# Six matmul steps of the last gate tile issued inside the first sample's latent attention, and that sample's key transposes issued two prompt steps earlier

## Chip, cores and metric

One core of a Trainium2 chip runs the whole kernel. The time is what the device needs for one execution, in microseconds (us). Each core has five engines with their own instruction streams: TensorE (PE, matmuls, with PEld its weight loads), VectorE (DVE), ScalarE (ACT), GpSimd (POOL) and SyncE (SP). They wait for one another on semaphores, and an instruction that waits holds up all that stands behind it on its engine.

## What is computed

One inference step of a decoder of two layers, for a prompt of 256 tokens and for 8 samples of 8 new tokens each, all in float32. A layer is a gated FFN, a mixing part, and a second gated FFN, with norms around each. The mixing part has three branches (a delta-rule recurrence A, a dilated window attention B, a latent attention C), and

```
gates = sigmoid(h @ w_in[gate columns] + b_gate)     # 3 x 1024 channels
m = gates[0] * (ya @ w_a) + gates[1] * (yb @ w_b) + gates[2] * (yc @ w_c)
x += post_mix(m @ w_out)
```

Branch C for a sample attends over 2048 past latent rows, which lie in pages that are gathered through a table, and over its own 8 tokens:

```
s = q_lat . ckv_all + q_rope . krope_all ;  p = softmax(s * scale) ;  o_lat = p @ ckv_all
```

## The kernel before, in words

The work of a layer is in one hand-written order on each engine: `ffn("f1")`, `a_proj`, `rwkv`, `bc_proj`, `sw_prompt`, `sw_sample`, `latent_prep`, `ml_prompt`, `ml_sample`, `mix`, `ffn("f2")`. The change touches the last part of `ml_prompt` (latent attention of the prompt) and the first of `ml_sample` (latent attention of the 8 samples).

**Dealt steps.** The gate and branch products are filler for PE. They are 40 tiles of 128 channels by 320 tokens: tiles 0 to 7 gate, 8 to 15 branch A, then 8 gate, 8 branch B, 8 gate. A gate tile is 8 steps (one matmul of 128x320 each over the 8 slices of the model width; a step shows as two MATMUL instructions in the trace), a branch tile 4, 256 steps in all (`N_DEAL`). `deal(count, cap)` issues the next `count` steps and stops at `cap`. Tile i accumulates in PSUM bank 6 + i % 2. The last step of a gate tile raises the semaphore `pgm`; ACT then takes the tanh of the tile (`gates_out`, L1660) and raises `gate`. So the 24th gate tile is done with `pgm` 24 and read out with `gate` 24. It lies in bank 7.

**ml_prompt.** `prompt(...)` runs 17 iterations n = 0 to 16 on PE: scores of unit n + 2, half of the dealt steps (3 of 6), values of unit n - 1, two transposes of unit n (L711), the other 3 steps. Before `ml_prompt` 154 steps have been dealt; the 17 times 6 here end at 256. In the last two iterations no scores are left. DVE (`prompt_attention`) runs i = 0 to 18: it masks and takes the maximum of unit i (L2256), divides unit i - 1 (L2289), copies the transposed shares of unit i - 2 (L2300), copies the output of unit i - 3 (L2271, `finish`, which raises `prompt_y`). At i = 17 and 18 it also calls `keys(0, 0)` and `keys(0, 1)`.

**keys(b, high)** (L2418) transposes the gathered pages of sample b in 32x32 blocks: two transposes of 128x1024 for the lower half of the latent channels, and two of 128x1024 and one of 128x512 for the upper half and the rotary keys. The lower half first waits for the three gathers of sample b (`s_kr`).

**ml_sample.** PE first waits for `prompt_y` 32, `ml_prep`, `gate` 24, `br_ev` and `s_ql`, then issues `own_tokens(0)` and for each sample b: `scores(b)`, `by_channel(b-2)`, `own_tokens(b+1)`, `values(b-1)`, `shares(b, 0)`, `shares(b, 1)`. `shares` transposes the exponentials (8 transposes, L711, and one small one, of the own tokens' shares, into bank 7 columns 448 to 511) and waits for `ml_exp` b + 1. The order on DVE is

```
own_scores(0)
for b in range(NB):
    if b:
        keys(b + 1, 0)
        divisor(b - 1)
    maximum(b)
    own_scores(b + 1)
    if b == 0:
        keys(1, 0)
    ...
    keys(b + 1, 1)
```

with `maximum` L2471 to L2477, `own_scores` L2466, `own_share` L2485 (after the keys; it raises `ml_p`, for which the small transpose waits), `divisor` L2490 to L2494. ACT takes the exponentials (L1736 and L1738), copies the outputs (L1744) and the transposed shares (L1749, L1750).

**Page gathers on POOL** (L690 the rotary keys, L693 two of latent rows; 3 per sample). There are four buffers; those of samples 2 and 3 lie in `ring` and `h`, and the first 4096 columns of `ring` hold the weights of the gate tiles 20 to 23 until `pgm` 24. POOL goes in this order, and the change leaves it as it is:

```
elif b == 1:
    pool.wait_ge(S["prompt_mm"], 2 * H + 16)
elif b in (2, 3):
    pool.wait_ge(S["prompt_y"], 2 * H + 16)
    pool.wait_ge(S["pgm"], 24)
else:
    pool.wait_ge(S["ml_pv"], b - 3)
```

(each of the first two with a wait for `ml_prep` too).

Of the kernel before, what the change touches and what calls it, by code (L numbers as in the profile page):

```python
# [189 lines left out]
N_DEAL = 2 * (64 + 32) + 64  # L190
# [78 lines left out]
def build(nc, io):  # L269
    SCB, SCC = DH ** -0.5, (DNOPE + DROPE) ** -0.5  # L270
    with ExitStack() as ctx:
# [150 lines left out]
        S = {n: sem(n) for n in STEPS}  # L422
# [275 lines left out]
        def _(pe):  # L698
# [396 lines left out]
            def prompt(base, scores, rows, count, cap):  # L1095

                def values(n):
                    hd, r0 = n % H, 64 * (n % 2)
                    pe.wait_ge(S["prompt_pt"], base + n + 1)
                    if n >= 2:  # L1100

                        pe.wait_ge(S["prompt_y"], base + n - 1)
                    for i in range(n // H + 1):
                        q = mm(ps[r0:r0 + 64, 5, P * (n % 2):P * (n % 2) + P], rows[:, i, hd * 64:hd * 64 + 64], PTp[n % 2][:, i, :], i == 0, i == n // H)
                    q.then_inc(S["prompt_o"], 1)

                scores(0)
                scores(1)
                for n in range(17):
                    if n + 2 < 16:  # L1110
                        scores(n + 2)
                    deal(count // 2, cap)
                    if n:
                        values(n - 1)
                    if n < 16:
                        pe.wait_ge(S["prompt_p"], base + n + 1)
                        for i in range(n // H + 1):
                            q = tr(ps[:, 4, i * P:i * P + P], Pc[n % 2][:, i * P:i * P + P])
                        q.then_inc(S["prompt_T"], 1)
                    deal(count - count // 2, cap)  # L1120

            def sw_prompt():
                pe.wait_ge(S["qk_ev"], 16)
# [204 lines left out]
            def ml_sample():  # L1328
                pe.wait_ge(S["prompt_y"], 2 * H + 16)
                pe.wait_ge(S["ml_prep"], 1)  # L1330
                pe.wait_ge(S["gate"], 24)
                pe.wait_ge(S["br_ev"], 2 * KD)

                pe.wait_ge(s_ql, 16 * 12)
# [17 lines left out]
                def own_tokens(b):  # L1352

                    if b >= NB:
                        return
                    if b:
                        pe.wait_ge(S["ml_own"], b)
                    if b >= 4:
                        pe.wait_ge(S["ml_olT"], b - 3)
                    o = ps[0:NS, 6, 0:TS]  # L1360
                    tk = slice(SEQ + TS * b, SEQ + TS * b + TS)
                    for c in range(2):
                        mm(o, QL[:, c, NS * b:NS * b + NS], ckvT[:, c, tk], c == 0, False)
                    mm(o, QR[64:96, b, :], ckvT[64:96, 2, tk], False, True).then_inc(S["ml_s"], 1)

                def shares(b, r):

                    if r == 0:
                        pe.wait_ge(S["ml_exp"], b + 1)
                    if b:  # L1370
                        pe.wait_ge(S["ml_pt"], 2 * b - 1 + r)
                    for u in range(4):
                        q = tr(ps[:, 4 + r, u * P:u * P + P], Pl[:, (4 * r + u) * P:(4 * r + u) * P + P])
                    if r:
                        pe.wait_ge(S["ml_p"], b + 1)
                        if b:
                            pe.wait_ge(S["ml_osb"], b)
                        q = tr(ps[0:NS, 7, 448:512], PnL, NS)
                    q.then_inc(S["ml_PT"], 1)
# [26 lines left out]
                for b in range(NB):  # L1406
                    scores(b)
                    by_channel(b - 2)
                    own_tokens(b + 1)
                    values(b - 1)  # L1410
                    for r in range(2):
                        shares(b, r)
# [60 lines left out]
        def _(act):  # L1473
# [179 lines left out]
            def gates_out(upto):  # L1653

                for n in range(gates_done[0], upto):
                    gates_done[0] = n + 1
                    bank = 6 + (n % 8 + 16 * (n // 8)) % 2
                    dst = (mt, gb, gc)[n // 8][:, n % 8, :]
                    act.wait_ge(S["pgm"], n + 1)
                    act.activation(dst, ps[:, bank, 0:T], ACT.Tanh, scale=0.5, bias=pp("b_gate", n)).then_inc(S["gate"], 1)  # L1660
# [60 lines left out]
            def ml_prompt():  # L1721
                for n in range(16):
                    act.wait_ge(S["prompt_nm"], 2 * H + n + 1)
                    scores = Sp[n % 2][:, 0, 0:(n // H + 1) * P]
                    act.activation(scores, scores, ACT.Exp, scale=SCC, bias=sml[:, 2 + n % 2:3 + n % 2], accum_out=sml[:, 4 + n % 2:5 + n % 2]).then_inc(S["prompt_e"], 1)
                    gates_out(complete(DEAL_AT["ml"] + DEAL_ML * n, "gate"))
                gates_out(24)

            def ml_sample():

                def exponentials(b):
                    act.wait_ge(S["ml_nm"], b + 1)
                    if b:

                        act.wait_ge(S["ml_PT"], 2 * b)
                    act.activation(Pl.rearrange("p (u i k) -> p i u k", u=8, i=4), ps[:, 0:4, 0:256].rearrange("p i (u k) -> p i u k", u=8),  # L1736
                                   ACT.Exp, scale=SCC, bias=sml[:, 4:5], accum_out=sml[:, 8:9])
                    act.activation(Pown[b % 2], Pown[b % 2], ACT.Exp, scale=SCC, bias=sml[0:NS, 4:5], accum_out=sml[0:NS, 10:11]).then_inc(S["ml_exp"], 1)  # L1738

                def output(b):  # L1740
                    if b < 0:
                        return
                    act.wait_ge(S["ml_pv"], b + 1)
                    act.activation(Osb, ps[:, 7, 0:KV_LORA], ACT.Copy).then_inc(S["ml_osb"], 1)  # L1744

                def shares_out(b, r):
                    act.wait_ge(S["ml_PT"], 2 * b + r + 1)
                    if r:
                        act.activation(PTl, ps[0:NS, 7, 448:512], ACT.Copy)  # L1749
                    act.activation(PTL[:, 4 * r:4 * r + 4, :], ps[:, 4 + r, :].rearrange("p (t n) -> p t n", t=4), ACT.Copy).then_inc(S["ml_pt"], 1)  # L1750

                for b in range(NB):
                    exponentials(b)
                    output(b - 1)
                    for r in range(2):
                        shares_out(b, r)
                output(NB - 1)
# [22 lines left out]
        def _(dve):  # L1780
# [480 lines left out]
            def prompt_attention(tag, y, one_group):  # L2261
# [13 lines left out]
                for i in range(19):  # L2275
# [25 lines left out]
                        dve.wait_ge(S["prompt_pt"], base + n + 1)  # L2301
                    if 3 <= i < 19:
                        finish(i - 3)
                    if one_group and i in (17, 18):
                        dve.wait_ge(S["pgm"], 20)
                        keys(0, i - 17)
                    branches_out(complete(DEAL_AT["ml"] + DEAL_ML * (i - 1), "branch") if one_group else min(KD, complete(DEAL_AT["sw"] + DEAL_SW * (i - 1), "branch")))

            branches_done = [0]
# [296 lines left out]
```

## Time and profile before

| | us |
|---|---|
| median of 3 runs | 2690.97 (2684.81 to 2694.35) |
| the profiled execution | 2691.49 |
| its span in the trace | 2689.6 |
| PE busy | 2589.1 (96%) |
| DVE busy | 1358.1 (50%) |
| ACT busy | 522.0 (19%) |
| POOL busy | 67.2 (2%) |

The span runs from the first to the last instruction that the profile records; the device time of the same execution is 1.9 us more. Busy time is an average over stages with different limits. The chain that ended last is followed back from the last instruction to what released each one; the timeline gives each engine's instructions in order of time, with the idle time before a group and what ended it in square brackets; times count from the start of the span. Layer 0's `ml_sample` begins near 936 us, layer 1's near 2269 us. PEclk in the table of windows is the granted clock of TensorE, 1.00 for 2.4 GHz and 0.50 for 1.2 GHz.

### The profile page before, as it was taken

The page shows a single profiled execution, that of the slowest core. Times are in us where ns is not written, and L with a number is a line of the kernel's source. Part 1 is how long each engine was busy: PE and PEld are TensorE (multiplying, and loading weights), DVE is VectorE, ACT ScalarE, POOL GpSimd, SP SyncE. Part 2 cuts the span into 40 slices and gives each one's busy share as a digit, 9 for nine tenths or more (in the row PEclk, how much of TensorE's full clock was granted, in tenths as well). Part 3 has the DMA queues.
Part 4 walks back from the last instruction along what each step waited for, and adds up shares of the span by engine and source line. Part 5 has one row for each costly group of instructions (what it writes and reads, how often), then busy time and mean ns, then how long its engine had stood idle before and what let it go on. Part 6 is the DMA issues. An engine that isn't in the chain of part 4 may idle for free.

```text
span 2689.6 us, 52084 instructions
## 1 busy us (share of the span) xinstructions
PE 2589.1 (96%) x22652; PEld 2042.4 (76%) x22652; DVE 1358.1 (50%) x2927; ACT 522.0 (19%) x1109; POOL 67.2 (2%) x92
## 2 busy tenths in 40 slices
PE   7999999999989999999999999999999899999998
PEld 6999656656656667899989996566566666779998
DVE  5663553436542482665376534533455435717653
ACT  2110131121432121211021111211224211312110
POOL 0000000000000110000000000000000001100000
PEclk9999999989999999999999999999999999999999
DMA  6435578631981379544534456684329614794442
GB/s 224 155 103 166 187 244 323 224 114 56 383 313 63 105 262 366 161 128 118 161 120 141 122 163 222 245 317 160 128 102 380 255 63 161 264 350 137 142 108 85
DMA packets 258754, 505.61 MB, mean 188 GB/s; under 512 B 9760, under 2 KB 196512, under 8 KB 243424
## 3 DMA queue, kind: packets, MB, share of 16 engines
q1 hardware_dynamic: 249824, 330.83, 37.4%
q0 software_dynamic: 8704, 171.45, 17.3%
q8 instruction: 180, 2.95, 0.4%
q14 instruction: 46, 0.38, 0.0%
HBM read 491.95 MB, written 140.85 MB: 235 GB/s over the span
## 4 chain that ended last, share of the span: by engine, by line
PE 90%; DVE 4%; ACT 2%; DMA 2%; issue 1%; SPq 0%; DVEq 0%; ACTq 0%
PE ps L708 84%; PE ps L711 6%; DMA ring<-in_w_in_dram 1%; DMA ring<-in_f_wu_dram 1%; ACT big L1680 1%; ACT reg L1680 0%; DMA big<-in_cache_swa_k_dram 0%; DVE reg L1843 0%; DVE reg L2053 0%; DVE x L1854 0%; SPq L572 0%; DVE ring L2380 0%; DVE big L2187 0%; DVE reg L2352 0%; ACT reg L1572 0%
## 5 line engine op out<-in xcount | busy, mean ns | idle before, releaser
L708 PE MATMUL ps<-reg 128*128 128x160 f32 (+12 forms) x4584 | 534.8, 292 | 3.1 <-issue 1.6
L708 PEld LDWEIGHTS ps<-reg 128*128 128x128 f32 (+5 forms) x4584 | 470.0, 163 | 50.5 <-issue 34.2
L708 PE MATMUL ps<-h,ring 128*128 128x320 f32 (+3 forms) x1792 | 464.7, 408 | 29.9 <-DMA ring<-in_f_wu_dram 13.8
L708 PE MATMUL ps<-reg,ring 128*128 128x160 f32 (+2 forms) x2912 | 458.2, 312 | 0.0
L708 PEld LDWEIGHTS ps<-reg,ring 128*128 128x128 f32 (+1 forms) x2912 | 415.5, 189 | 26.7 <-issue 6.2
L708 PEld LDWEIGHTS ps<-h,ring 128*128 128x128 f32 (+2 forms) x1792 | 311.6, 194 | 134.4 <-issue 45.5
L708 PE MATMUL ps<-ring,h 128*128 128x512 f32 (+3 forms) x896 | 249.9, 474 | 2.7 <-DMA ring<-in_w_in_dram 2.7
L708 PE MATMUL ps<-big,ring 64*64 64x64 f32 (+3 forms) x1920 | 231.7, 292 | 12.3 <-ACT big L1502 6.7
L708 PEld LDWEIGHTS ps<-big,ring 128*128 128x128 f32 (+1 forms) x1920 | 189.2, 165 | 63.3 <-issue 39.9
L708 PEld LDWEIGHTS ps<-ring,h 128*128 128x128 f32 (+1 forms) x896 | 104.0, 165 | 83.6 <-issue 64.6
L708 PE MATMUL ps<-big,reg 32*64 32x256 f32 (+8 forms) x2144 | 132.1, 346 | 0.0
L708 PEld LDWEIGHTS ps<-big,reg 32*64 32x64 f32 (+4 forms) x2144 | 101.7, 134 | 23.8 <-issue 14.8
L711 PE MATMUL ps<-cst,big 128*128 128x128 f32 (+1 forms) x672 | 98.8, 284 | 17.6 <-ACT big L1680 7.3
L708 PE MATMUL ps<-ring 128*16 128x128 f32 (+3 forms) x1888 | 98.7, 272 | 3.2 <-DVE ring L2380 3.2
L711 PEld LDWEIGHTS ps<-cst,big 128*128 128x128 f32 (+1 forms) x672 | 72.3, 140 | 38.4 <-ACT big L1680 12.4
L708 PEld LDWEIGHTS ps<-ring 128*16 128x16 f32 (+3 forms) x1888 | 76.9, 116 | 25.0 <-issue 18.6
L711 PE MATMUL ps<-cst,reg 128*128 128x128 f32 (+3 forms) x436 | 73.7, 289 | 12.7 <-ACT ring L1738 6.1
L708 PE MATMUL ps<-ring,reg 32*64 32x256 f32 (+2 forms) x1312 | 81.8, 398 | 0.0
L1547 ACT ACTIVATE reg<-ps 128x320 f32<-128x320 f32 x40 | 17.5, 437 | 323.1 <-PE ps L708 323.1
L708 PE MATMUL ps<-ys,ring 128*128 128x320 f32 x256 | 77.4, 437 | 0.0
L711 PEld LDWEIGHTS ps<-cst,reg 128*128 128x128 f32 (+3 forms) x436 | 50.5, 143 | 34.3 <-issue 12.9
L1982 DVE TENSOR_TENSOR ys<-ys,ps 128x320 f32<-128x320 f32 x40 | 19.5, 488 | 109.7 <-PE ps L708 109.6
(311 smaller groups left out, 2673.1 us busy)
## 6 DMA issues: line engine op xcount, KB each, us to landing
out_o_swa_k_s_dram<-in_cache_swa_k_dram POOLq DMA_DIRECT2D x16, 4080.0 KB, 15.6
out_o_swa_v_s_dram<-in_cache_swa_v_dram POOLq DMA_DIRECT2D x16, 4080.0 KB, 16.6
ring<-in_w_in_dram SPq DMA_DIRECT2D x30, 2048.0 KB, 8.7
ring<-in_f_wd_dram SPq DMA_DIRECT2D x32, 1408.0 KB, 7.2
ring<-in_f_wg_dram SPq DMA_DIRECT2D x42, 1024.0 KB, 5.4
ring<-in_f_wu_dram SPq DMA_DIRECT2D x42, 1024.0 KB, 8.1
big<-in_cache_swa_k_dram SPq DMA_DIRECT2D x32, 1024.0 KB, 8.4
ring<-in_cache_swa_v_dram SPq DMA_DIRECT2D x32, 1024.0 KB, 6.9
```

The costliest lines, as they stand in the source:

```text
L708: return pe.matmul(out, lhsT, rhs, start=first, stop=last, skip_group_check=True)
L711: return pe.transpose(out, in_, ident[0:rows, 0:rows])
L1547: act.activation(GU[u % 2][:, :, 0, 0:HT], summed(X), ACT.Copy).then_inc(S["gu_act"], 1)
L1680: act.activation(KTw[n % 2][:, c, 0:w], ps[:, 4 + c % 2, 0:w], ACT.Copy).then_inc(S["kt_act"], 1)
L1982: dve.tensor_tensor(Vs, Xc, Y, ALU.add).then_inc(S["gu_sum"], 1)
```

## The change

Both calls of `deal` in `prompt` stop six steps earlier when they serve `ml_prompt`. The six steps (2 to 7 of the last gate tile) are issued in `ml_sample`, after `scores(0)` and `own_tokens(1)` and ahead of `shares(0, 0)`. The wait for `gate` 24 ahead of `ml_sample` becomes one for 23, and a wait for 24 stands ahead of the small transpose of sample 0, which writes the same bank. ACT reads the tile out after sample 0's exponentials. DVE issues `keys(0, 0)` and `keys(0, 1)` at i = 15 and 16.

```diff
@@ prompt, PE
-                    deal(count // 2, cap)
+                    deal(count // 2, cap - (6 if cap == N_DEAL else 0))
...
-                    deal(count - count // 2, cap)
+                    deal(count - count // 2, cap - (6 if cap == N_DEAL else 0))
@@ ml_sample, PE
-                pe.wait_ge(S["gate"], 24)
+                pe.wait_ge(S["gate"], 23)
...
                     if r:
                         pe.wait_ge(S["ml_p"], b + 1)
+                        if b == 0:
+                            pe.wait_ge(S["gate"], 24)
...
                     own_tokens(b + 1)
+                    if b == 0:
+                        deal(N_DEAL)
                     values(b - 1)
@@ ml_prompt, ACT
-                gates_out(24)
+                gates_out(23)
@@ ml_sample, ACT
                     exponentials(b)
+                    if b == 0:
+                        gates_out(24)
                     output(b - 1)
@@ prompt_attention, DVE
-                    if one_group and i in (17, 18):
+                    if one_group and i in (15, 16):
                         dve.wait_ge(S["pgm"], 20)
-                        keys(0, i - 17)
+                        keys(0, i - 15)
```

## Rows read from the trace of the kernel before

**Rows 1.** The page's first part, the whole span: busy time, share, instructions.
```profile
PE 2589.1 (96%) x22652; PEld 2042.4 (76%) x22652; DVE 1358.1 (50%) x2927; ACT 522.0 (19%) x1109; POOL 67.2 (2%) x92
```

**Rows 2.** The chain that ended last, both layers: start us, us, what.
```profile
935.09 0.78 issue
...
956.92 9.37 PE ps L708 x188
...
2267.79 0.78 issue
...
2291.10 9.16 PE ps L708 x187
```

**Rows 3.** Timeline, layer 0, end of ml_prompt and first sample: start us, us, what.
```profile
921.66 0.28 DVE L2271 COPY ys<-ps 64x128 f32<-64x128 f32 x1
...
925.85 0.29 DVE L2271 COPY ys<-ps 64x128 f32<-64x128 f32 x1
...
929.30 3.40 PE L708 MATMUL ps<-h,ring 128*128 128x320 f32 x12
929.57 0.42 DVE L2300 COPY ring<-ps 128x256 f32<-128x256 f32 x1 [3.43 <-PE ps L711]
...
930.35 2.37 DVE L2418 STREAM_TRANSPOSE ring<-big 128x1024 f32<-128x1024 f32 x2
...
932.63 0.65 PE L708 MATMUL ps<-ring 128*64 128x128 f32 x4
...
933.21 1.88 PE L708 MATMUL ps<-h,ring 128*128 128x320 f32 x6
933.32 0.29 DVE L2271 COPY ys<-ps 64x128 f32<-64x128 f32 x1 [0.60 <-PE ps L708]
933.65 2.97 DVE L2418 STREAM_TRANSPOSE big<-big 128x1024 f32<-128x1024 f32 x3
935.13 0.53 ACT L1660 ACTIVATE ys<-ps,par 128x320 f32<-128x320 f32 x1 [4.56 <-PE ps L708]
```

**Rows 4.** Timeline, PE's hole in the first sample of layers 0 and 1.
```profile
943.97 1.09 PE L711 MATMUL ps<-cst,reg 128*128 128x128 f32 x8 [3.06 <-ACT ring L1738]
...
2276.94 1.97 PE L711 MATMUL ps<-cst,reg 128*128 128x128 f32 x8 [3.02 <-ACT ring L1738]
```

**Rows 5.** Timeline of POOL: gathers of sample 2, layer 0 (first, third), layer 1 (first).
```profile
935.89 0.95 POOL L690 DMA_INDIRECT ring<-in_cache_mla_krope_dram,pidx  x1 [13.66 <-PE ps L708]
...
938.39 0.94 POOL L693 DMA_INDIRECT ring<-in_cache_mla_ckv_dram,pidx  x1 [0.30 <-issue]
...
2268.59 0.95 POOL L690 DMA_INDIRECT ring<-in_cache_mla_krope_dram,pidx  x1 [13.65 <-PE ps L708]
```

**Rows 6.** DMA queues: sample 1's bytes; its third gather, us to landing; all of layer 0.
```profile
q0 software_dynamic: 368, 2.36, 56.6%
...
reg<-in_cache_mla_ckv_dram,pidx POOLq DMA_INDIRECT x1, 7.8
...
DMA to landing us min/median/max: 6.4/7.2/8.2
```

**Rows 7.** Timeline, second sample: DVE's keys of sample 2, the maximum, what follows.
```profile
947.96 2.33 DVE L2418 STREAM_TRANSPOSE ring<-ring 128x1024 f32<-128x1024 f32 x2
...
951.43 1.20 DVE L2473 TENSOR_REDUCE sml<-ps 128x1 f32<-128x1024 f32 x1
951.48 3.67 PE L708 MATMUL ps<-big,reg 128*64 128x256 f32 x32
...
956.68 0.10 PEld L711 LDWEIGHTS ps<-cst,ring 64*64 64x64 f32 x1 [0.17 <-DVE ring L2485]
...
2285.32 1.23 DVE L2473 TENSOR_REDUCE sml<-ps 128x1 f32<-128x1024 f32 x1 [0.85 <-PE ps L708]
```

**Rows 8.** Windows: us, PE, PEld, DVE, ACT, POOL busy, PEclk, DMA share, GB/s.
```profile
944.00:949.00 5.00, 4.97 (x89) 3.40 (x97) 4.96 (x6) 1.30 (x3) 0.00 (x0) 0.66 1.02 428
2276.00:2284.00 8.00, 7.06 (x121) 5.02 (x129) 7.82 (x12) 2.18 (x7) 0.00 (x0) 0.57 0.94 371
1087.00:1092.00 5.00, 4.53 (x11) 2.98 (x12) 4.95 (x13) 5.00 (x13) 0.00 (x0) 0.66 0.93 298
...
2421.00:2427.00 6.00, 5.49 (x21) 3.93 (x22) 5.00 (x13) 6.00 (x16) 0.00 (x0) 1.00 0.87 285
```

## The prediction, made before the changed kernel was run

> **What bounds the kernel now.** The page's first part comes first: PE is busy in 96% of the span [rows 1], so time is saved where PE stands idle or runs at the lower clock, and lost where it gets a new wait. The chain that ended last shows the two places at the seam of `ml_prompt` and `ml_sample` (layer 0; layer 1 repeats it). PE waits 0.78 us at 935.09 [rows 2], for the tanh of gate tile 23 at 935.13 [rows 3]. Then, after scores(0) and own_tokens(1), it is idle 3.06 us up to 943.97 until ACT's exponentials are there; layer 1 has 3.02 us [rows 4]. The change aims at both: six steps are to leave the first place and fill the second. The windows show what else the hole costs: in the stretches behind it the granted clock is 0.66 over 5 us and 0.57 over 8 us [rows 8], that is partly the 1.2 GHz level. Last the timeline of POOL and DVE, for all that waits for the steps that move: POOL issues sample 2's gathers at 935.89, 0.80 us after the dealt steps' end at 935.09 [rows 2, 5]. It cannot go before `pgm` 24.
>
> **Removed from the prompt's end.** The group of 12 matmuls at 929.30 is six steps, two instructions a step; three of them stay, three go. values(15) followed it at 932.63 [rows 3], so twelve take 3.33 us and values(15) moves 1.66 us forward, to 930.97. The 6 matmuls of 933.21 (1.88 us) go too. What then releases `ml_sample` is DVE's copy of values(15), at 933.32 for 0.29 us [rows 3]: now done at 931.95. I add 0.25 us for the wait's release and the satisfied waits behind it (after the tanh's end at 935.66, PE needed 0.21 to 935.87 [rows 2, 3]). PE starts `ml_sample` at 932.20 instead of 935.87: **3.67 us earlier**. The wait for `gate` 23 costs nothing; that tile is finished before the moved tile's first step.
>
> **Keys at i = 15 and 16.** 2.37 and 2.97 us of DVE [rows 3] stand now behind the output copies that end at 921.94 and 926.14. The first lasts to 924.31, the division of unit 15 moves behind it, and PE asks for that only at its transposes near 929. The second ends at 929.11, and DVE's next copy starts at 929.57 [rows 3]. Cost: nothing, hidden by DVE's idle 3.43 us; with that cover gone it would be at most these 5.3 us. They also no longer hold up anything at the end; the page wait of sample 0 and `pgm` 20 are long met.
>
> **Added in the first sample.** own_tokens(1) ended at 943.97 - 3.06 = 940.91, now at 937.24. Six steps take 1.88 + 1.66 = 3.54 us, to 940.78. The exponentials are there at 943.97 - 3.67 = 940.30, so the first shares come 0.5 us later than they could. ACT's tanh (0.53 us) fits behind the exponentials, before the first copy of shares. If nothing else happened, sample 1 would begin some 3.2 us earlier and at full clock.
>
> **What is late next: the pages of sample 2.** `pgm` 24 now comes at 940.78 where it came at 935.09. With the same 0.80 us lag POOL's first gather starts at 941.58, 5.7 us later than in the old kernel, while all else is 3.7 us earlier. The third gather starts 938.39 - 935.89 = 2.50 us behind the first [rows 5]. It has no landing time in the trace, so I take its nearest neighbour, the third gather of sample 1, of equal shape: 7.8 us [rows 6]. Together 10.3 us after the first issue: 951.88. The ends are 9.7 (median 7.2) and 10.7 (maximum 8.2) [rows 6]. The check on it: in the old kernel this gives 946.2, and DVE did take up these pages at 947.96 with no idle time [rows 7].
>
> DVE meets keys(2, 0) in sample 1's turn **ahead of** divisor(0) and maximum(1). Queued behind that wait are the maximum, so ACT's exponentials, so PE's shares(1), own_share(1) and with it scores(2). From the start of keys(2, 0) to the maximum is 951.43 - 947.96 = 3.47 us [rows 7]: now at 951.88 + 3.47 = 955.35, **3.92 us later than in the old kernel**. The small transpose ahead of scores(2) was waiting for DVE [rows 7], so scores(2), at 956.92 [rows 2], follows the maximum by 5.49 us: 960.84, +3.92.
>
> Layer 1: the hole ended 2276.94 - 3.02 = 2273.92, so the pieces there are 0.3 us longer. First gather at 2268.59 + 5.69 + 0.31 = 2274.59 [rows 5], pages at 2284.89, maximum at 2288.36 where it was 2285.32 [rows 7], scores(2) at 2293.85 where it was 2291.10 [rows 2]: +2.75. It is less because the old maximum waited 0.85 us for a slow-clocked PE.
>
> **The clock.** PE has finished values(0) near 950.4 (scores(1) starts near 942 and takes some 4.1 us at full clock, own tokens 0.5, values 3.67 [rows 7]) and stands idle until the exponentials at about 958.8: 8 us instead of 3. After the 3 us holes the clock rows lost (1 - 0.66) x 5 = 1.7, (1 - 0.57) x 8 = 3.4 with 0.9 of idle in it, and 1.7 us [rows 8]; a fourth stretch, 2421 to 2427, behind a like pause, shows 1.00 and lost nothing. The old holes' loss is already in the old times above, since the new wait swallows whatever is gained before it. The new hole's loss comes on top, less what passes while DVE is still at work on sample 2's keys, some 2 us of clock time. Bounds 0 and 2.4 us a layer; I take 1.3, between, since a longer pause is nearer to the stretches that lost.
>
> **Sum.** +3.92 + 2.75 + 2 x 1.3 = +9.3 us on the profiled execution's 2691.49, that is 2700.8; the median stands 0.5 lower, so **2700.3**. From there on each sample is PE's own pace (9.37 us of matmuls without a break in the chain [rows 2]), so nothing is caught up. Ends: stalls of 3.3 + 2.1 with landing at 9.7, less 0.5 each if POOL's lag is nearer to 0.3, and no clock loss: +4.4. Stalls of 4.3 + 3.2 and 2.4 twice: +12.3.
>
> **Rivals.** (B) The hole is filled and the pages don't matter. Then DVE reaches maximum(1) 3.67 us earlier in layer 0 and, free of the slow PE, 4.6 in layer 1, and scores(2) follows: -3.7 and -4.9, together -8.6 us, 2682.4. It decides at the start of keys(2, 0): the pages would have to be there at 947.96 - 3.67 = 944.29, 2.7 us after the first issue. Break-even is 947.96. For it: the hole and the low clock are real [rows 4, 8]. Against it: 2.36 MB [rows 6] at 428 GB/s [rows 8] alone take 5.5 us. Only if I misread which gather is held by `pgm` 24 does it stand. Chance 0.10.
> (C) The gathers land much sooner than sample 1's, because they overlap. If all three are there 7.2 us after the first issue, the median of a single one [rows 6], the pages come at 948.78 and 2281.79, the maximum at 952.25 (+0.8) and 2285.26 (-0.1); with 2.6 of clock that is +3.3, 2694.3 for the median. At the bound of 5.5 us the maximum is 0.9 and 1.8 us earlier than in the old kernel, and with 0 to 2.6 us of clock the time is 2688 to 2691. For it: the lag of the first bytes may hide behind the other gathers. Against it: sample 1's own three landings. Chance 0.10, all within 0.3%.
> The Trainium skill (DMA: Bandwidth & Descriptors, Anatomy of one DMA) has a transfer issued by GpSimd take 2.0 us plus its bytes at 436 GB/s. For 2.36 MB that is an estimate of 7.4 us in place of 10.3, and 2694.7 in place of 2700.3. The trace disagrees with it for sample 1's gathers: three issues 1.25 us apart put the last landing at 10.3.
> (A) is my forecast, the chain as worked out: chance 0.80.
>
> **From cases to numbers.** About 0.3%, 8.1 us, is what a measurement of this kernel can tell from no change: the lines are 2682.9 and 2699.0. (A) runs from 2695.4 to 2703.3; two thirds of it lies over 2699.0 (clock loss of over some 1.4 us in all, at the middle stalls): slower 0.52, same 0.28. (C) adds 0.10 to same. (B) lies on the lower line: 0.07 faster, 0.03 same. The range takes in (A), (C)'s upper half and about a microsecond of scatter: 2691 to 2705.
>
> **What would show it.** Right, if in the new trace POOL's first gather of sample 2 starts near 941.6 and 2274.6; DVE waits for DMA for some 7 us before keys(2, 0) in both layers; maximum(1) starts near 955.4; PE is idle about 8 us ahead of shares(1) with a lower clock behind it; and `ml_sample` begins near 932.2. The key transposes at i = 15 and 16 should move no PE row. Wrong, if DVE goes into keys(2, 0) without idle time, if the hole at 943.97 stays, if ml_sample starts no earlier, or if later samples run faster than before and win the stall back.

## The result, and the profile after

The changed kernel is slower: 2703.61 us, the median of 20 executions, beside 2695.11 for 20 of the old kernel on the same chip. The ratio on record is 1.0048 [1.0032, 1.0064], that is +13 us, from +9 to +17. It is not the quotient of the two medians, which is 1.0032 (+8.5 us); in the runs below the two also differ, by up to 0.2%. Every ratio here is the one on record, with its interval. The profiled execution took 2702.42 us, 10.9 more than the one of before. The forecast was +9.3 us on that execution; its time, 2700.3, is 3.3 us under the median measured now. It was built on a median of 3 executions, 2690.97, which stands 4.1 us under that of 20.

The page's first part, of the changed kernel (beside [rows 1]):

```profile
PE 2587.9 (96%) x22652; PEld 2042.3 (76%) x22652; DVE 1357.3 (50%) x2927; ACT 521.2 (19%) x1109; POOL 67.3 (2%) x92
```

No engine has more or less to do. What was added is waiting, and the timeline of layer 0 has it. (Line numbers in the kernel after are 4 higher in ACT's part and 6 higher in DVE's.)

```profile
923.93 0.42 DVE L2306 COPY ring<-ps 128x256 f32<-128x256 f32 x1 [0.37 <-PE ps L711]
...
926.55 0.40 PE L708 MATMUL ps<-reg 128*64 128x8 f32 x4 [0.46 <-DVE ys L2277]
...
931.55 3.50 PE L708 MATMUL ps<-h,ring 128*128 128x320 f32 x12
...
934.89 1.04 PE L711 MATMUL ps<-cst,reg 128*128 128x128 f32 x8
935.09 0.53 ACT L1664 ACTIVATE ys<-ps,par 128x320 f32<-128x320 f32 x1 [0.46 <-PE ps L708]
...
935.85 0.95 POOL L690 DMA_INDIRECT ring<-in_cache_mla_krope_dram,pidx  x1 [19.19 <-PE ps L708]
936.03 1.98 PE L708 MATMUL ps<-ring,reg 32*64 32x256 f32 x64
...
938.35 0.94 POOL L693 DMA_INDIRECT ring<-in_cache_mla_ckv_dram,pidx  x1 [0.30 <-issue]
...
946.73 2.37 DVE L2424 STREAM_TRANSPOSE ring<-ring 128x1024 f32<-128x1024 f32 x2 [7.98 <-DMA ring<-in_cache_mla_ckv_dram,pidx]
...
950.23 1.21 DVE L2479 TENSOR_REDUCE sml<-ps 128x1 f32<-128x1024 f32 x1
...
953.72 1.97 PE L711 MATMUL ps<-cst,reg 128*128 128x128 f32 x8 [8.38 <-ACT ring L1742]
...
955.86 3.71 PE L708 MATMUL ps<-ring,reg 32*64 32x256 f32 x64
```

Read from above: `ml_sample` starts (926.55) as soon as DVE has copied values(15); the twelve matmuls of the moved steps stand where the hole of [rows 4] was, and the shares follow them without idle time (934.89). POOL's first gather of sample 2 comes 0.8 us behind the steps. DVE then stands 7.98 us before it may transpose sample 2's first keys, maximum(1) queues behind that, and PE is idle 8.38 us. The 64 matmuls that take 1.98 us at 936.03 take 3.71 at 955.86. The chain that ended last has the gathers in it, which that of before has not:

```profile
935.85 0.79 POOL ring L690
936.64 0.47 issue
937.11 0.94 POOL ring L693
938.05 0.30 issue
938.35 8.35 DMA ring<-in_cache_mla_ckv_dram,pidx
```

Layer 1 repeats it (timeline; beside the last lines of [rows 5, 4, 7]):

```profile
2270.80 0.95 POOL L690 DMA_INDIRECT ring<-in_cache_mla_krope_dram,pidx  x1 [19.18 <-PE ps L708]
...
2284.90 1.21 DVE L2479 TENSOR_REDUCE sml<-ps 128x1 f32<-128x1024 f32 x1
...
2288.39 1.97 PE L711 MATMUL ps<-cst,reg 128*128 128x128 f32 x8 [8.10 <-ACT ring L1742]
```

The windows behind the new holes (columns as in [rows 8]). While PE takes up work again, at 953.72, the granted clock is 0.50, the 1.2 GHz level. In the next 5 us it is 0.60, and 0.54 in layer 1: still the lower level for most of the time. The 5 us after these are at full clock in both layers.

```profile
951.00:956.00 5.00, 2.28 (x17) 1.83 (x25) 4.78 (x12) 2.38 (x7) 0.00 (x0) 0.50 1.02 424
956.00:961.00 5.00, 5.00 (x120) 3.38 (x128) 2.84 (x8) 0.67 (x2) 0.00 (x0) 0.60 0.05 20
2290.00:2295.00 5.00, 5.00 (x99) 3.08 (x103) 3.47 (x11) 0.84 (x3) 0.00 (x0) 0.54 0.20 82
```

**A ruler for the seam.** Two executions drift apart by some microseconds before the seam is reached, with the same code (its first mark below stands at 929.57 in the old trace and at 923.93 in the new). So all that follows counts from DVE's copy of unit 15's transposed shares, the first line of the timeline above. Each column is the start of one line of the timeline, less that mark, layer 0 / layer 1; max(b) is DVE's maximum of sample b, "wait" DVE's idle time for sample 2's pages. "Gather 2" is POOL's first gather of sample 2, and SP's first transfer in the two plain kernels. The number behind a name is the chip's.

| kernel, chip | ml_sample | gather 2 | max(0) | max(1) | max(2) | wait |
|---|---|---|---|---|---|---|
| before, first pair | 6.3 / 6.3 | 6.3 / 6.3 | 10.9 / 11.2 | 21.9 / 23.1 | 31.5 / 33.0 | 0 |
| after, first pair | 2.6 / 2.6 | 11.9 / 11.9 | 7.2 / 7.2 | 26.3 / 26.0 | 38.2 / 37.9 | 8.0 / 7.7 |
| again2 (= after), 7 | 2.6 | 11.9 | 7.3 / 7.3 | 26.2 / 26.2 | 38.2 / 38.1 | 7.9 / 7.9 |
| thin_base, 7 | 6.3 | 6.3 | 10.9 / 10.9 | 22.7 / 21.9 | 32.7 / 31.7 | 0 |
| thin_after, 7 | 2.6 | 11.9 | 7.3 / 7.2 | 22.2 / 22.2 | 33.5 / 32.7 | 3.9 / 3.9 |
| late_order, 7 | 5.5 | 10.9 | 10.2 / 10.1 | 20.9 / 20.9 | 33.3 / 33.3 | 0 |
| plain_base, 8 | 6.3 | 5.6 | 10.9 / 13.1 | 22.7 / 24.0 | 32.7 / 33.7 | 0 |
| plain_after, 8 | 2.6 | 11.2 | 7.2 / 7.2 | 24.0 / 24.1 | 35.3 / 35.3 | 5.5 / 5.8 |
| base (= before), 11 | 6.3 | 6.3 | 19.1 / 19.3 | 30.8 / 31.2 | 42.9 / 43.3 | 0 |
| keys_only, 1 | 6.4 | 6.4 | 19.1 / 19.2 | 31.0 / 31.1 | 43.0 / 43.1 | 0 |
| again (= after), 1 | 2.6 | 11.9 | 7.3 / 7.3 | 26.0 / 24.9 | 39.0 / 36.8 | 7.7 / 6.5 |
| late_gather, 1 | 6.3 | 11.7 | 10.9 / 10.9 | 25.0 / 25.2 | 35.7 / 35.0 | 3.0 / 3.3 |
| free_pages, 1 | 2.6 | 2.8 | 15.2 / 15.6 | 26.2 / 26.6 | 36.8 / 37.2 | 0 |

### The profile page after: what moved, and what is told of

Read it like the earlier page. It is cut to its first block, busy times and chain, and to the rows that moved or that the text cites. A ratio compares the mean times of both kernels' runs of the same rounds, so it can differ in the third digit from the quotient of the medians.

```text
span 2700.5 us, 52086 instructions
## 1 busy us (share of the span) xinstructions
PE 2587.9 (96%) x22652; PEld 2042.3 (76%) x22652; DVE 1357.3 (50%) x2927; ACT 521.2 (19%) x1109; POOL 67.3 (2%) x92
## 3 DMA queue, kind: packets, MB, share of 16 engines
q1 hardware_dynamic: 249824, 330.83, 37.2%
## 4 chain that ended last, share of the span: by engine, by line
PE 90%; DVE 4%; ACT 2%; DMA 1%; issue 1%; SPq 0%; POOL 0%; DVEq 0%; POOLq 0%; ACTq 0%
PE ps L708 85%; PE ps L711 6%; DMA ring<-in_f_wu_dram 1%; DMA ring<-in_cache_mla_ckv_dram,pidx 1%; ACT big L1684 1%; ACT reg L1684 0%; DVE ring L2386 0%; DVE reg L1849 0%; DVE reg L2059 0%; DVE x L1860 0%; DVE big L2193 0%; DVE ring L2424 0%; SPq L572 0%; DVE reg L2358 0%; ACT reg L1576 0%
## 5 line engine op out<-in xcount | busy, mean ns | idle before, releaser
L711 PE MATMUL ps<-cst,reg 128*128 128x128 f32 (+3 forms) x436 | 73.6, 288 | 23.3 <-ACT ring L1742 16.5
```

The costliest lines, as they stand in the source:

```text
L711: return pe.transpose(out, in_, ident[0:rows, 0:rows])
```

## Experiments

Theory P, the forecast's: the pages of sample 2 come late, and that is the loss. Its rival R (S in the expectations): the moved steps, or the keys in their new place, cost in themselves. Where an expectation names a time without a chip, it goes by the first pair.

### First group: the pages, the keys, and the kernel itself

**again** is the changed kernel, unchanged, for a common footing.

> The changed kernel once more. Theory P (late pages): DVE waits for sample 2's pages for about 8 us in both layers, and the maximum of sample 2 starts 38.4 us after the last full group of dealt steps where it was 31.8 in the old kernel (33.3 in layer 1); 9 to 14 us slower than the old kernel. What the changed kernel's layer 1 lost beyond that (PE's issue gaps of 2.58 and 0.6 us in samples 6 and 7) is there again if it belongs to the change, and absent or elsewhere if it is scatter of one execution.

Measured: 2723.98 beside 2730.09 for the old kernel, ratio 0.9976 [0.9958, 0.9994]. The sign is turned, and both kernels are 20 to 35 us slower than in the first pair.

**keys_only**: the old kernel with `i in (15, 16)` and `keys(0, i - 15)`.

> The old kernel with DVE's key transposes of sample 0 at i = 15 and 16 and nothing else. Both theories: the start of ml_sample hangs on the tanh of the last gate tile, so nothing moves on PE: within 1 us of the old kernel. If the earlier transposes did hold PE up in the prompt's last units, it would show here as 1 us or more.

Measured: 2735.06, 0.9999 [0.998, 1.0018]. The seam stands where it stands in base, to 0.2 us, so no cost of the keys' new place shows; the interval of the time is some 5 us to either side.

**late_gather**: the old kernel, with POOL's gathers of sample 2 held back as the change does, and no step moved:

```diff
                         pool.wait_ge(S["pgm"], 24)
+                        pool.wait_ge(S["ml_mm"], 1)
```

> The old kernel, no step moved; POOL's gathers of samples 2 and 3 also wait for the end of sample 0's scores, some 4.7 us later than before. Theory P: pages near 951.2 in the old kernel's clock instead of 946.2, maximum of sample 1 some 3.3 us later than in the old kernel, a second hole of PE of 3 to 5 us ahead of its shares and low clock behind it: 5 to 11 us slower in all, though nothing but the gathers is late. Rival S (the moved steps themselves, or the cover they gave, cost the time): no change within 1 us.

Measured: 2722.18, 0.9968 [0.9949, 0.9988]. The wait for the pages is there (3.04 us), and yet it is faster, where 5 to 11 us of loss were expected.

**free_pages**: the changed kernel, where the last six steps no longer read the slot that sample 2's pages are to fill, so that POOL may go at once:

```diff
-                        pool.wait_ge(S["pgm"], 24)
+                        pool.wait_ge(S["pgm"], 23)
...
+                        if n >= N_DEAL - 6:
+                            q = mm(out, kvup[1][:, 0:P], x[:, k, :], ...)
```

> The changed kernel, but the six moved steps multiply other data that lie in SBUF anyway (lora's first 128 columns and x), and POOL's gathers of samples 2 and 3 wait for pgm 23; the last gate tile's values are other ones. Same matmuls in the same places, pages free of them. Theory P: no wait for pages before keys(2, 0), no hole of 3 us in sample 0 and no low clock behind it: 7 to 11 us faster than the old kernel, so some 20 faster than the changed one. Rival S: as slow as the changed kernel.

Measured: 2721.02, 0.9959 [0.9941, 0.9977], and no page wait; but max(0) comes at 15.2 instead of 7.3.

What follows: on this chip, gathers issued early cost time in the first sample, gathers issued late cost a wait in the second. In the old kernel max(0) is at 19.1 here and 10.9 in the first pair, with the same code. That cost wasn't in either theory. So this group does not tell P from R for the loss of the first pair.

### Second group: a second chip of this kind, and the order of DVE

**base** is the old kernel, with a profile.

> The old kernel, for its trace beside the others of this group. After the first group there are two theories. P (late pages): the wait of DVE for sample 2's pages is what the change costs. F (starved PE): PE's own instructions come slowly while page gathers run, which shows as idle time ended by issue between small groups of weight loads; in the kernel with only the keys moved this held the scores of sample 0 up by 8 us, in the changed kernel the gathers start after these scores. F expects on a chip that behaves as that one: the first maximum 19 us after the copy of unit 15, later samples 12.7 us apart. On one that behaves as in the first two traces: 10.9 us, and 10.6 us apart.

Measured: 2732.82, 0.9993 [0.9973, 1.0012]. Its timeline of POOL and of PE's weight loads shows the loss:

```profile
932.69 0.95 POOL L690 DMA_INDIRECT ring<-in_cache_mla_krope_dram,pidx  x1 [13.65 <-PE ps L708]
...
938.94 0.94 POOL L693 DMA_INDIRECT h<-in_cache_mla_ckv_dram,pidx  x1 [0.30 <-issue]
```

```profile
933.02 1.18 PEld L708 LDWEIGHTS ps<-ring,reg 32*64 32x64 f32 x38
934.74 0.22 PEld L708 LDWEIGHTS ps<-ring,reg 32*64 32x64 f32 x6 [0.54 <-issue]
935.50 0.23 PEld L708 LDWEIGHTS ps<-ring,reg 32*64 32x64 f32 x6 [0.54 <-issue]
936.97 0.20 PEld L708 LDWEIGHTS ps<-ring,reg 32*64 32x64 f32 x4 [1.25 <-issue]
...
940.62 0.17 PEld L708 LDWEIGHTS ps<-big,reg 32*64 32x64 f32 x1 [0.45 <-issue]
941.33 0.81 PEld L708 LDWEIGHTS ps<-big,reg 32*64 32x64 f32 x23 [0.53 <-issue]
```

From 1.5 us after POOL's first gather has started to 1.5 us after its last has ended, PE gets a handful of matmuls at a time, then 0.45 to 1.25 us nothing, and waits for no engine ("issue"). In the first pair the same scores run beside gathers with no such gap: 64 matmuls in 1.98 us at 936.03, in the first timeline.

**order**: the changed kernel, DVE's maximum(1) and own_share(1) put ahead of keys(2, 0):

```diff
-                        keys(b + 1, 0)
+                        if b != 1:
+                            keys(b + 1, 0)
...
-                    if b == 0:
-                        own_share(0)
+                    if b < 2:
+                        own_share(b)
+                    if b == 1:
+                        keys(2, 0)
```

> The changed kernel with one more edit on DVE: in sample 1's turn keys(2, 0) stands behind the maximum and own_share(1) instead of ahead of them. Theory P: DVE still waits for the pages, but the maximum of sample 1 comes some 6 to 8 us earlier, PE's hole ahead of shares(1) goes, and a shorter one of 2 to 4 us stands ahead of scores(2): 4 to 6 us per layer faster than the changed kernel, 8 to 12 in all. If the time is lost elsewhere: no change against the changed kernel.

Measured: 2725.71, 0.9964 [0.9945, 0.9982]. The page wait is gone, but max(1) comes at 24.7 and 25.1 where again, on chip 1, had 26.0 and 24.9. The expected 6 to 8 us are missed: it is 1.3 us sooner in layer 0 and no sooner in layer 1. DVE now waits for PE, whose scores(1) stand in the gathers' stretch:

```profile
949.44 1.23 DVE L2479 TENSOR_REDUCE sml<-ps 128x1 f32<-128x1024 f32 x1 [8.61 <-PE ps L708]
```

**steps_only**: the changed kernel with the keys back at i = 17 and 18.

> The changed kernel with the key transposes of sample 0 back at i = 17 and 18. They stand ahead of the copy of unit 15 that releases ml_sample and ahead of scores(0)'s upper half: ml_sample starts some 1 us later and scores(0) waits for keys: the first maximum 1 to 3 us later than in the changed kernel, and the gathers' start with it; 2 to 4 us slower than the changed kernel.

Measured: 2724.18, 0.997 [0.9954, 0.9986]. Here the keys do matter: `ml_sample` starts at 3.5 instead of 2.6 and max(0) comes at 8.5 instead of 7.3, but the page wait (7.0 us) swallows it. In their new place the keys hold nothing up: in the first timeline DVE even stands idle for 0.37 us behind them, ahead of the copy at 923.93. In the old place they would hold the earlier seam up by 1.2 us.

**tanh_wait**: the old kernel with the keys at 15 and 16 and the wait for tile 23 instead of 24 ahead of `ml_sample` (24 only ahead of the small transpose); no step moved.

> The old kernel with its keys at i = 15 and 16 and PE's wait for the last gate tile's tanh moved behind the shares of sample 0, all steps where they were. pgm 24 and the gathers come when they came, ml_sample starts 0.5 to 0.8 us earlier: 1 to 1.5 us faster than the old kernel in all, nothing else moves. It takes the part of the gain that does not delay the pages.

Measured: 2729.81, 0.9985 [0.9965, 1.0004]: not told apart from no change. In its trace `ml_sample` starts at 5.5 instead of 6.3, POOL's gather stays at 6.4. That is 0.8 us a layer, the issue row of [rows 2]; at max(0) 0.3 to 0.5 us of it are left (18.8 beside base's 19.1 and 19.3).

### Third group: a chip like the first pair's

**thin_base** and **thin_after**: the kernels before and after, the latent-row gathers of samples 2 and 3 replaced by as many gathers of 2 KB rows, so that a third of sample 2's bytes is left, with the same issues. What these two samples attend to is then wrong.

```diff
+                        if b in (2, 3):
+                            pool.indirect_dma_start(out=KRc[b % 4][half][:, 0:2, :]..., in_=krope, in_offset=rows_of(0))
+                            continue
```

> The old kernel, but the latent-row gathers of samples 2 and 3 fetch 2 KB a row from the rotary-key cache in place of 8 KB of latent rows (0.79 MB a sample, not 2.36); the rest of these two samples' pages is stale, so the two samples' attention is not computed from their keys. As many gathers, issued at the same times, with a third of the bytes. Theory F says that bytes in flight starve PE's instruction supply: on a chip like that of the groups before, the first maximum comes 11 to 14 us after the copy of unit 15 instead of 19.1, in both layers, and the kernel is 10 to 16 us faster than the old one. If the issue on POOL or the number of gathers did it: 19, and no faster.

Measured: 2692.78, 0.9995 [0.9967, 1.0023].

> The changed kernel with the same thin gathers for samples 2 and 3. The pages land some 6 us after the first issue instead of 10.7. Theory P: DVE's wait shrinks to about 2 to 3 us, the second maximum comes about 21 us after the copy of unit 15 instead of 24.9 to 26, and PE's issue gaps in sample 1's scores shrink too; 4 to 10 us faster per layer than the changed kernel. Against thin_base: 3 us faster to 2 us slower per layer, the change's own worth when the pages cost little.

Measured: 2696.75, 0.9996 [0.9972, 1.002].

**again2** is the changed kernel.

> The changed kernel beside these. If this chip behaves as in the last two groups: 4 to 9 us faster than the old kernel, page wait of DVE 6.5 to 8 us in both layers. If as in the first two traces: 9 to 15 us slower.

Measured: 2709.39, 1.0046 [1.0021, 1.007].

This chip runs the old kernel in 2693.71 and repeats the first pair's 1.0048. The timeline of DVE, first in again2 and then in thin_after:

```profile
949.60 2.37 DVE L2424 STREAM_TRANSPOSE ring<-ring 128x1024 f32<-128x1024 f32 x2 [7.87 <-DMA ring<-in_cache_mla_ckv_dram,pidx]
```

```profile
941.58 2.37 DVE L2428 STREAM_TRANSPOSE ring<-ring 128x1024 f32<-128x1024 f32 x2 [3.89 <-DMA ring<-in_cache_mla_krope_dram,pidx]
```

Same steps, same keys, same order, fewer bytes (sample 3's too): the wait is 4.0 us shorter, max(1) is 4.0 us earlier, and the ratio falls from 1.0046 to 0.9996, no longer told apart from no change. The thin gathers alone gain nothing (thin_base, 0.9995). That decides for P. By rival R both should have lost the same, since both have the moved steps. A small rest may stay: max(2) of thin_after is 0.8 and 1.0 us behind thin_base's. The size fits too: of sample 2's 2.36 MB [rows 6] a third stays, so 1.6 MB fewer are moved. They would take 3.9 us at the 403 GB/s of this window, from the changed kernel of the first pair:

```profile
943.00:948.00 5.00, 2.34 (x20) 1.07 (x16) 1.27 (x2) 0.00 (x0) 1.92 (x3) 1.00 1.01 403
```

**late_order**: the old kernel with the keys at 15 and 16, tanh_wait's edit, late_gather's wait and order's order of DVE; the six steps stay in `ml_prompt`.

> A candidate: the steps stay in the prompt, the tanh wait moved behind sample 0's shares, keys at i = 15 and 16, gathers of samples 2 and 3 held until sample 0's scores are done, and keys(2, 0) behind the maximum of sample 1. Theory F with P: the scores of sample 0 run unhindered (first maximum at 10.1), the gathers run in the hole and in sample 1's scores, whose slow pace now takes the place of DVE's wait: 8 to 12 us faster than the old kernel here, like late_gather or 1 to 2 us better.

Measured: 2694.79, 0.9994 [0.997, 1.0017]. Gathers late, no page wait, and no loss that can be told (the interval runs from 8 us faster to 5 slower; max(2) is at 33.3, beside 32.7 and 31.7 in thin_base). That fits the reading that a gather held back costs because keys(2, 0) stands ahead of the maximum. It does not show it by itself: the kernel has three more edits, and late_gather, which holds the gathers back in the old order, was not run on a chip of this kind.

### Fourth group: why the second kind of chip is slow there

Two theories for the gaps of base: F, the gathers' bytes crowd the fetching of PE's instructions; G, POOL's issuing of indirect gathers does, whatever they carry. **thin_base2**, **thin_after2**, **order2** and **late_order2** are the kernels of those names again, on chip 11.

> The thin gathers in the old kernel again (a third of the bytes for samples 2 and 3, whose attention is not computed from their keys). On a chip of the second kind, theory F: first maximum 11 to 14 us after the copy of unit 15 instead of 19.1. If not the bytes but the gathers' issue starves PE: 17 to 19. On one of the first kind it has shown 10.9 and will again, no faster than the old kernel.

Measured: 2731.56, 1.0 [0.9984, 1.0016]; max(0) at 19.4, as with all bytes. The weight loads:

```profile
932.60 1.19 PEld L712 LDWEIGHTS ps<-ring,reg 32*64 32x64 f32 x38
934.32 0.22 PEld L712 LDWEIGHTS ps<-ring,reg 32*64 32x64 f32 x6 [0.54 <-issue]
935.08 0.22 PEld L712 LDWEIGHTS ps<-ring,reg 32*64 32x64 f32 x6 [0.54 <-issue]
936.55 0.20 PEld L712 LDWEIGHTS ps<-ring,reg 32*64 32x64 f32 x4 [1.25 <-issue]
```

The same gaps, to the hundredth, with a third of the bytes: F falls.

> The thin gathers in the changed kernel again. On a chip of the first kind: second maximum at 22.2 as before, 3.9 us of page wait, 4 to 12 us faster than the changed kernel. On one of the second kind, theory F: second maximum at 22 to 24 instead of 25 to 26, 4 to 14 us faster than the changed kernel.

Measured: 2722.7, 0.9976 [0.9958, 0.9993]; page wait 3.3 and 3.2 us, max(1) at 25.2 and 24.8 where again had 26.0 and 24.9: with fewer bytes it is hardly sooner, and in front of it DVE waits for PE (3.2 us in layer 1), not for pages.

> The changed kernel with keys(2, 0) behind sample 1's maximum and own_share(1). On a chip of the first kind (10.9 us from the copy of unit 15 to the first maximum in the old kernel), theory P: second maximum 16 to 18 us after that copy instead of 26.2, third near 34 instead of 38.2, PE waits 2 to 5 us for the keys ahead of sample 2's scores; 6 to 10 us faster than the changed kernel, so within 5 us of the old one. On a chip of the second kind: as before, 25 and 37 to 39, 6 to 12 us faster than the old kernel.

Measured: 2726.5, 0.9993 [0.9972, 1.0014], beside 0.9964 for the same kernel two groups before: the two intervals only just overlap, and I take order as somewhere between them.

> The candidate with the steps in the prompt, late gathers of samples 2 and 3 and keys(2, 0) behind the maximum. On a chip of the second kind: first maximum at 10.1 instead of 19.1, second at 24 to 26, 8 to 12 us faster than the old kernel. On one of the first kind: first maximum at 10.1, second at 20.9, third at 33.3, within 3 us of the old kernel.

Measured: 2716.02, 0.9951 [0.9935, 0.9968], the lowest ratio on this kind of chip, though its interval overlaps with those of order, late_gather and steps_only: max(0) at 10.1 where base has 19.1, and no page wait.

### Fifth group: the same bytes without POOL

**plain_base** and **plain_after**: SP's plain transfers of fixed rows stand in for POOL's gathers of samples 2 and 3, behind the same marks. Their attention is computed from other rows.

```diff
+                        sp.wait_ge(S["pgm"], 24)
+                        for b in (2, 3):
+                            sp.dma_start(KRr[b], rope_rows[P * b:P * b + P, :])
...
-                for b in range(NB):
+                for b in (0, 1, 4, 5, 6, 7):
```

> The old kernel; samples 2 and 3 get their pages by six plain transfers that SP issues at the point where POOL issued its gathers, of the same sizes, from fixed rows (so these two samples' attention is computed from other rows). Theory G: it is POOL's issue of indirect gathers that slows PE's instruction supply. Then on a chip of the second kind the first maximum comes at 10.9 us after the copy of unit 15 instead of 19.1 to 19.4, in both layers, and the kernel is 12 to 17 us faster than the old one; sample 4 and later stay 12.7 us apart since POOL gathers their pages still. If any transfer of these bytes does it: 17 to 19. On a chip of the first kind: 10.9 and within 3 us of the old kernel.

Measured: 2695.5, 0.9999 [0.9976, 1.0022].

> The changed kernel with the same plain transfers for samples 2 and 3. They still wait for pgm 24. Theory P with G, on a chip of either kind: first maximum at 7.25, DVE waits for sample 2's pages as long as the transfers take, which for plain ones of 2.36 MB beside 2.36 MB more is 6 to 10 us after the first issue: second maximum 21 to 25 us after the copy of unit 15 and PE idle 3 to 8 us ahead of shares(1); against plain_base 0 to 8 us slower in all. If the change were a gain wherever gathers don't slow PE, it would be faster than plain_base.

Measured: 2699.54, 1.0015 [0.9995, 1.0035].

The group fell on chip 8, which is like the first pair (old kernel 2695.67, plain_base's max(0) at 10.9), so it says nothing about G; **G stays open**. What it does show: issued by SP, the three transfers follow one another faster and the wait is 5.5 us (timeline of DVE in plain_after), and the ratio lies between that of a 3.9 us wait and that of 7.9.

```profile
946.89 2.37 DVE L2433 STREAM_TRANSPOSE ring<-ring 128x1024 f32<-128x1024 f32 x2 [5.54 <-DMA ring<-in_cache_mla_ckv_dram]
```

So on chips of the first kind four kernels stand in order of their page wait: 0 us (late_order) 0.9994, 3.9 us 0.9996, 5.5 us 1.0015, 7.9 us 1.0046. Only the last is clear of no change; the order of the other three lies inside their intervals. As I read it, and it is not shown, the first 4 us are paid by the earlier start and the filled hole, and past that the change loses.

## What the prediction had right, and the step that failed

The forecast (A) names the mechanism that the runs showed, on chips of the first pair's kind. **What failed is a size in the sum: the clock term, "2 x 1.3".** It took 1.3 us a layer, the middle of its bounds of 0 and 2.4; measured were 2.2 and 1.9 us, 1.5 us more in all. The landing, 10.3 us, was too short as well (10.9 and 10.6), which adds 0.5 us in layer 0. At the third maximum the new kernel is 11.6 us late in the trace, where the sum gave 9.3; the ratio on record says 13. By its own steps, times from the mark:

- **`ml_sample` 3.67 us sooner.** Forecast at 2.63, measured 2.62. Right.
- **Keys at 15 and 16 cost nothing.** Right: keys_only shows no cost, and DVE's idle 0.37 us behind them none in the new kernel. That they also free the end of the prompt was said without a number; steps_only gives it, 1.2 us.
- **The deal in the hole.** 3.50 us where 3.54 was worked out. I said that the shares would be up to 0.5 us late; they start as the steps end, and the old hole is gone.
- **First gather 5.7 us later.** Forecast at 12.0, measured 11.9 in both layers.
- **Landing 10.3 us after the first issue.** Measured 946.73 - 935.85 = 10.9, and 10.6 in layer 1. This is a term that was sized too small: its neighbour took 7.8 us from the third issue, this one 8.35 and 8.1. The upper end given was 10.7. The neighbour, sample 1's gather, had no other gathers behind it; sample 2's have sample 3's three. That this is the reason for the longer landing is argued, not shown. Rival (C), which rested on a landing of 7.2, fell. By the Trainium skill (DMA: Bandwidth & Descriptors, Anatomy of one DMA) the estimate, with the three gathers taken as one transfer, was 7.4 us; the trace disagrees in both layers.
- **Maximum(1).** Forecast at 25.8 and 26.1, measured 26.3 and 26.0: +4.4 and +3.0 us on before, against +3.9 and +3.0.
- **The clock, 1.3 us a layer.** From max(1) to max(2) the old kernel took 9.7 and 10.0 us, the new one 11.9 in both layers: 2.2 and 1.9 us more. This is the step that failed. The rows of layer 0, the old kernel's first and then the new one's:

```profile
956.85 1.98 PE L708 MATMUL ps<-ring,reg 32*64 32x256 f32 x64
...
958.63 1.93 PE L708 MATMUL ps<-big,reg 32*64 32x256 f32 x64
...
961.10 1.22 DVE L2473 TENSOR_REDUCE sml<-ps 128x1 f32<-128x1024 f32 x1 [0.86 <-PE ps L708]
```

```profile
959.33 2.25 PE L708 MATMUL ps<-big,reg 32*64 32x256 f32 x64
...
962.14 1.22 DVE L2479 TENSOR_REDUCE sml<-ps 128x1 f32<-128x1024 f32 x1 [3.10 <-PE ps L708]
```

  Scores(2) of the new kernel loses 3.71 - 1.98 = 1.7 us on its first 64 matmuls and 2.25 - 1.93 = 0.3 on the next 64, together 2.0 of the 2.2. The windows say the same: (1 - 0.60) x 5 = 2.0 us, and (1 - 0.54) x 5 = 2.3 in layer 1. The prediction set off some 2 us of low clock that pass while DVE works on sample 2's keys. They did pass there (0.50 in the window from 951 to 956), but the low clock lasted on into scores(2). The two pauses, 8.38 and 8.10 us, are the longest of PE in this trace.
- **The sum.** At max(2) the new kernel is +6.7 and +4.9, together 11.6 us late, where the steps gave 9.3. The measured ratio, 1.0048, is +13, with 9 to 17 as its bounds: the forecast is near the lower one. That 2700.3 lies close to the measured median is in part luck, since the two medians are only 8.5 us apart and the forecast's base stood 4.1 us low.
- **"From there on each sample is PE's own pace."** In layer 0 it holds: the new kernel is 6.7 us late at max(2) and 6.7 at max(7), so nothing is caught up. In layer 1 it fails as a statement: 4.9 us at max(2) become 11.6 at max(7). The chain after, in layer 1, has gaps in PE's issue:

```profile
2317.76 0.59 issue
...
2339.68 2.58 issue
...
2360.62 0.61 issue
```

Such gaps also come in thin_base, where nothing of the change is (max(5) to max(6) takes 16.5 us in its layer 1 and 10.6 in its layer 0), and in plain_base. Of the eight traces from chips of the first kind, six have them in layer 1 (14.5 to 17.1 us from max(5) to max(6)) and none in layer 0; the two without are before and late_order. So they don't need the change. Whether it makes them more frequent can't be told from eight traces, and their cause stays open. They are part of why one pair of profiles can't be summed to a microsecond: up to max(7) the two layers are 18.3 us late together, and the whole execution only 10.9, so that the rest of it took 7.4 us less.

Rival (B), a gain of 8.6, needed pages that don't matter. It fell on the first pair. free_pages is as near as the runs came to it, on the other kind of chip: there too the early gathers have a price.

What the prediction did not have at all is the **chip**. On chip 1 the changed kernel is faster, 0.9976; by itself it was not run on chip 11, where with thin gathers it has the same ratio. On both chips the old kernel, or the old kernel with the keys moved, loses 8 us a layer in scores(0), because the six gathers are issued beside it (max(0) at 19.1 instead of 10.9). The change, and late_gather alone, moves those gathers behind scores(0). The slow stretch then falls on scores(1), where PE is early and DVE waits for the pages anyway, and max(1) stands at 26.0 and 24.9, no later than on the other chips. So the wait of P is still there, and the gain is larger. The trace of before was one of a chip where none of this shows.

**A version worth keeping.** late_order is level with the old kernel on chip 7 and 0.5% faster on chip 11. Against the changed kernel it is ahead on chip 7, 2694.79 beside 2709.39. On the other kind of chip it stands at 0.9951 on chip 11 and the changed kernel at 0.9976 on chip 1; the intervals overlap, and the two were not run on one chip. Not tried: late_gather on a chip of the first kind, which would show the late pages by themselves, and order on such a chip, where it would keep the earlier start of `ml_sample` as well.

## What to carry to other kernels

When a step is moved, look for whatever waits for its last read: here six cheap steps held the slot that a gather fills, and 3.5 us of work put into a 3 us hole cost 0.5% of the kernel on one kind of chip. In an engine's written order, put what others are waiting for ahead of what itself waits for a transfer; with that order, in late_order, no cost of the late gather could be told. And a verdict under half a per cent can hang on the chip: take it from more than one before it is believed.

## What the runs showed of the hardware that was not expected

- The same kernel takes 2693.71 and 2695.67 us on chips 7 and 8, and 2729.91 to 2732.56 on chips 1 and 11. Part of the difference is the stretch beside the gathers: 8 us a layer in scores(0), and later samples 12.7 us apart (base) instead of 10.6.
- On chips 1 and 11, while POOL issues indirect gathers, PE's weight loads come some six at a time with gaps of 0.45 to 1.25 us between, with all of sample 2's and 3's bytes and with a third of them. That POOL's issuing is the cause fits all windows seen (the gaps follow the gathers in base, again, order and free_pages) and is argued, not shown: the run without POOL landed on a chip that has no such gaps. Nor can it be the cause of all of them: in the changed kernel of the first pair PE stands 2.58 us in "issue" at 2339.68, and POOL's last indirect gather was issued at 2327.07.
- Three gathers in series, 2.36 MB, took 10.6 to 10.9 us from the first issue to the last landing; with a third of the bytes 6.8 (thin_after, 941.58 less its first issue at 934.79).
- After 8 us without work PE took up its matmuls at a granted clock of 0.50 (window 951 to 956). In the 5 us from 956 and from 2290, which start 2.3 and 1.6 us after PE's restart, it was 0.60 and 0.54. The third maximum came 2.2 and 1.9 us later by it.
